# First norm's weights loaded as columns, x scaled and rounded in smaller steps, and the first products taken by two contraction chunks between the turns of x

## What is computed

```python
def rms_norm(x, g):
    xf = x.astype(jnp.float32)
    y = xf * lax.rsqrt(jnp.mean(jnp.square(xf), axis=-1, keepdims=True) + EPS)
    return (y * g.astype(jnp.float32)).astype(x.dtype)
...
qkv_raw, z, b, a, q_down, kv_down, gates = jnp.split(
    rms_norm(x, norm_mix) @ w_in, IN_SPLITS, axis=-1)
```

## Time and profile before

| | |
|---|---|
| median of 3 runs | 1457.36 us (1457.14 to 1457.37) |
| span of the profiled execution | 1455.6 us |
| PE busy | 1445.4 us (99%) |
| ACT busy | 868.4 us (60%) |
| DVE busy | 808.5 us (56%) |
| POOL busy | 217.1 us (15%) |
| granted clock of PE in 40 equal slices | 90% or more in each |
| chain that ended last | PE 96%, DVE 2% |

### The profile page before, as it was taken

One profiled execution on the slowest core, in us unless ns is written; L12 is line 12 of the kernel. 1 busy time (PEld: TensorE's weight loads), 2 busy tenths in 40 slices (PEclk: granted clock), 3 DMA queues, 4 the chain that ended last, 5 costly groups with the idle time before them and its releaser, 6 DMA issues.

```text
span 1455.6 us, 28542 instructions
## 1 busy us (share of the span) xinstructions
PE 1445.4 (99%) x10052; PEld 1182.0 (81%) x10052; DVE 808.5 (56%) x1664; ACT 868.4 (60%) x2816; POOL 217.1 (15%) x111
## 2 busy tenths in 40 slices
PE   9999999999999999999999999999999999999998
PEld 7877777877777777778777787777778999999998
DVE  5865445555546564555655555645434766777643
ACT  5545678686666686575855667766775353344332
POOL 3001111111122111111221111122122000000000
PEclk9999999999999999999999999999999999999999
DMA  9541315653245534365333453333734465555551
GB/s 280 172 119 30 83 26 117 156 116 70 63 102 123 121 86 86 74 132 125 85 70 82 113 139 70 63 70 73 189 77 152 145 235 183 168 172 191 181 174 59
DMA packets 263720, 173.61 MB, mean 119 GB/s; under 512 B 165464, under 2 KB 212088, under 8 KB 263576
## 3 DMA queue, kind: packets, MB, share of 16 engines
q1 hardware_dynamic: 263266, 171.53, 45.3%
q10 hardware_dynamic: 318, 0.33, 0.1%
HBM read 132.22 MB, written 6.74 MB: 95 GB/s over the span
## 4 chain that ended last, share of the span: by engine, by line
PE 96%; DVE 2%; ACT 0%; DMA 0%; ACTq 0%; issue 0%; POOL 0%; DVEq 0%
PE ps L2016 17%; PE ps L2018 16%; PE ps L2017 16%; PE ps L2453 6%; PE ps L2454 6%; PE ps L2455 6%; PE ps L2056 2%; PE ps L2037 2%; PE ps L2109 2%; PE ps L2401 2%; PE ps L2402 2%; PE ps L2110 2%; PE ps L2403 2%; PE ps L2111 2%; PE ps L1894 2%; PE ps L2046 1%
## 5 line engine op out<-in xcount | busy, mean ns | idle before, releaser
L851 ACT ACTIVATE ksq<-ps 128x128 f32<-128x128 f32 x1024 | 268.1, 277 | 279.5 <-PE ps L2018 278.0
L2016 PE MATMUL ps<-ukh,cTh 128*128 128x512 f32 x1024 | 418.4, 409 | 0.3 <-DVE cTl L1236 0.3
L2018 PE MATMUL ps<-ukh,cTl 128*128 128x512 f32 x1024 | 400.7, 391 | 0.0
L2017 PE MATMUL ps<-ukl,cTh 128*128 128x512 f32 x1024 | 399.9, 391 | 0.0
L705 POOL TENSOR_TENSOR rk<-kss,mhalf 128x32 f32<-128x32 f32 x32 | 180.1, 5628 | 478.0 <-DVE kss L1684 478.0
L2016 PEld LDWEIGHTS ps<-ukh,cTh 128*128 128x128 f32 x1024 | 192.6, 188 | 55.8 <-issue 17.1
L2018 PEld LDWEIGHTS ps<-ukh,cTl 128*128 128x128 f32 x1024 | 192.2, 188 | 42.9
L2017 PEld LDWEIGHTS ps<-ukl,cTh 128*128 128x128 f32 x1024 | 192.8, 188 | 34.0
L851 ACT ACTIVATION_READ_ACCUMULATOR ksq<-ps 128x1 f32 x1024 | 212.2, 207 | 0.0
L839 ACT ACTIVATE cTr<-turned 128x1024 uint16<-128x1024 uint16 x126 | 173.8, 1379 | 10.9 <-PE ps L2040 5.7
L1236 DVE TENSOR_TENSOR cTl<-cTr,cTh 128x512 fp32r<-128x512 f32 x128 | 88.4, 691 | 136.9 <-ACT cTh L842 136.0
(11 more groups left out here) (514 smaller groups left out, 2590.7 us busy)
## 6 DMA issues: line engine op xcount, KB each, us to landing
clat<-cache_mla SPq DMA_DIRECT2D x128, 256.0 KB, 2.6
wraw<-w_in SPq DMA_DIRECT2D x16, 1024.0 KB, 5.1
wraw<-w_up SPq DMA_DIRECT2D x16, 1024.0 KB, 5.4
wraw<-w_down SPq DMA_DIRECT2D x16, 1024.0 KB, 5.0
braw<-w_in SPq DMA_DIRECT2D x24, 512.0 KB, 4.0
crope<-cache_mla SPq DMA_DIRECT2D x128, 32.0 KB, 2.4
sst<-state_gdn SPq DMA_DIRECT2D x32, 128.0 KB, 3.2
gdn_sample<-sst SPq DMA_DIRECT2D x32, 128.0 KB, 2.0
```

The source lines that it names most:

```text
L851: i = nc.scalar.activation(ksq[:, P * h:P * h + P], ps[:, k % 3, P * h:P * h + P], ACT.Square, accum_out=kss[:, n // 4 % 2, n % 4, 4 * hal ...
L2016: mm(out, cTh[:, n % 2, c], ukh[:, c, cols], start=c == 0, stop=False)
L2017: mm(out, cTh[:, n % 2, c], ukl[:, c, cols], start=False, stop=False)
L2018: i = mm(out, cTl[:, n % 2, c], ukh[:, c, cols], start=False, stop=c == 3)
```

## The change

Four things are changed, all within the front.

1. `norm_mix` is loaded once more, straight as columns into a small tile `mixp` (128 partitions by 8), by a DMA that ACT issues second. Each of its 1,024 numbers is a piece of 4 bytes by itself. `x_normed` reads `mixp` and no longer `par`.
2. x is scaled and rounded in three steps, of two, two and four chunks (`XQ`), and ACT rounds weight piece 0 in two steps of two contraction chunks each (`first_hi`). `lo(0)` is still one step.
3. PE's order: six chunks of x are turned, then comes one more unused matmul into bank 4, then the high products of half unit 0 for contraction chunks 0 and 1 (`first_products(0)`), then x chunks 6 and 7, then the high products for chunks 2 and 3.
4. The turn of `prow` goes behind those products and waits until ACT has copied chunk 7; its copy to `par` stands on DVE between `x_low(1)` and `lo(1)`.

```diff
@@ ACT
             act.dma_start(consts[:, 0:C_COS.start], C_in[:, 0:C_COS.start]).then_inc(S("consts_landed"), 16)
+            act.dma_start(mixp[:], I["norm_mix"].rearrange("l (c p) -> p (l c)", p=P), allow_slow_non_contiguous=True).then_inc(S("mix_landed"), 16)
...
-            def x_high(half):
-                act.wait_ge(S("x_made"), half + 1)
-                nc.scalar.activation(Ah[:, 4 * half:4 * half + 4, :], xn[:, 4 * half:4 * half + 4, :], ACT.Copy).then_inc(S("left_hi"), 1)
+            def x_high(k):
+                act.wait_ge(S("x_made"), k + 1)
+                nc.scalar.activation(Ah[:, XQ[k], :], xn[:, XQ[k], :], ACT.Copy).then_inc(S("left_hi"), 1)
+
+            def first_hi(kc):
+                act.wait_ge(S("w_landed0"), landed[0])
+                nc.scalar.activation(hi_of(0)[:, kc, :], wraw[:, 0, kc], ACT.Copy).then_inc(S("w_hi0"), 1)
 
             x_chunk(1)
+            first_hi(slice(0, 2))
+            x_high(0)
             x_chunk(3)
-            hi(0)
-            x_high(0)
+            first_hi(slice(2, 4))
+            x_high(1)
+            act.wait_ge(S("w_hi0"), 2)
+            act.sem_inc(S("w_hi"), 1)
             x_chunk(5)
             x_chunk(7)
             hi(1)
...
@@ DVE
+            def x_normed(k):
+                n_ = XQ[k].stop - XQ[k].start
+                v.wait_ge(S("mix_landed"), 16)
+                v.wait_ge(S("x_even"), XQ[k].stop // 2)
+                v.wait_ge(S("x_odd"), XQ[k].stop // 2)
...
             x_chunk(0)
+            x_normed(0)
             x_chunk(2)
-            v.wait_ge(S("side_done"), side("params"))
-            V.tensor_copy(par[:, 0:PR_ALL], ps[:, 4, 0:PR_ALL]).then_inc(S("side_read"), 1)
-            x_normed(0)
+            x_normed(1)
             x_chunk(4)
             x_chunk(6)
             x_low(0)
             lo(0)
-            x_normed(1)
+            x_normed(2)
             x_low(1)
+            v.wait_ge(S("side_done"), side("params"))
+            V.tensor_copy(par[:, 0:PR_ALL], ps[:, 4, 0:PR_ALL]).then_inc(S("side_read"), 1)
             lo(1)
...
@@ PE
+            def first_products(k):
+                pe.wait_ge(S("w_hi0"), k + 1)
+                pe.wait_ge(S("left_hi"), k + 1)
+                for j in range(4):
+                    half_products(0, 0, 0, hi_of, Ah, j, (2 * k, 2 * k + 1))
+
+            def params_turned():
+                pe.wait_ge(S("params_landed"), 16 * 12)
+                pe.wait_ge(S("x_odd"), 4)
+                nc.tensor.transpose(begin("params")[:, 0:PR_ALL], prow[0:PR_ALL, :], ident[0:PR_ALL, 0:PR_ALL]).then_inc(S("side_done"), 1)
+
+            for c in range(6):
+                x_turned(c)
+            mm(ps[:, 4, :], warm[:, 0:P], warm[:, P:P + 512], start=True, stop=True)
+            pe.wait_ge(S("x_even"), 2)
+            pe.wait_ge(S("x_odd"), 2)
+            first_products(0)
+            x_turned(6)
+            x_turned(7)
+            first_products(1)
```

More of the change, by code:

```diff
@@ L257, in build @@
         assert e <= PERSIST
+        mixp, _ = place("mixp", [P, KC], F32, 212800 - 64)
         warm, _ = place("warm", [P, 640], F32, taken["qr"][0])
@@ L449, in z_columns @@
             return 1024 * 3 + 512 * (i // 2) if i < 4 else OFF_GATES + 512 * ((i - 4) // 2)
+        XQ = [slice(0, 2), slice(2, 4), slice(4, 8)]
         SLOT = {0: 0, 1: 1, 3: 0, 6: 1, 7: 0, 8: 1, 9: 0, 10: 1}
@@ L774, in _ @@
             square(sq[:, 0:8, :], xT[:], "sq_ready")
-            x_high(1)
+            x_high(2)
             hi(2)
@@ L800, in _ @@
                 drain(5, j, 12 + j, kn[:, 4 + j, :])
-            act.wait_ge(S("x_made"), 3)
+            act.wait_ge(S("x_made"), 4)
             nc.scalar.activation(rsq[:, 1], rsq[:, 0], ACT.Sqrt).then_inc(S("sqrt_done"), 1)
@@ L1141, in x_chunk @@
                 V.tensor_copy(xT[:, c, :], ps[:, XBANK[c], 0:T]).then_inc(S("x_even"), 1)
[L1143 to L1148, removed]
+            def x_normed(k):
[3 more added lines that the diff above has]
+                v.wait_ge(S("x_odd"), XQ[k].stop // 2)
+                V.tensor_tensor(xn[:, XQ[k], :], xT[:, XQ[k], :], mixp[:, XQ[k]].unsqueeze(2).to_broadcast([P, n_, T]), ALU.mult).then_inc(S("x_made"), 1)
             def x_low(half):
                 cs = slice(4 * half, 4 * half + 4)
-                v.wait_ge(S("left_hi"), half + 1)
+                v.wait_ge(S("left_hi"), half + 2)
                 V.tensor_tensor(Al[:, cs, :], xn[:, cs, :], Ah[:, cs, :].bitcast(F32), ALU.subtract).then_inc(S("left_lo"), 1)
             x_chunk(0)
+            x_normed(0)
             x_chunk(2)
-            v.wait_ge(S("side_done"), side("params"))
-            V.tensor_copy(par[:, 0:PR_ALL], ps[:, 4, 0:PR_ALL]).then_inc(S("side_read"), 1)
-            x_normed(0)
+            x_normed(1)
             x_chunk(4)
@@ L1188, in _ @@
             lo(6)
-            v.wait_ge(S("left_hi"), 4)
+            v.wait_ge(S("left_hi"), 5)
             V.tensor_tensor(qdl[:], qd[:], qdh[:].bitcast(F32), ALU.subtract).then_inc(S("left_lo"), 1)
@@ L1886, in unit, with half_products @@
                         beside(j)
+            def half_products(n, q0, half, w, x, j, kcs=range(4), last=False):
+                for kc in kcs:
+                    i = mm(ps[:, (q0 + j) % 4, 0:T], w(n)[:, kc, 128 * j:128 * j + 128], x[:, 4 * half + kc, :], start=w is hi_of and x is Ah and half == 0 and kc == 0, stop=last and kc == 3)
+                return i
             def half_unit(n, q0, half, beside=None):
[L1890 to L1902, removed]
+                if n > 0:
+                    pe.wait_ge(S("w_hi"), n + 1)
+                    pe.wait_ge(S("left_hi"), half + 2)
+                    for j in range(4):
+                        if half == 0:
+                            bank(q0 + j)
+                        half_products(n, q0, half, hi_of, Ah, j)
                 if beside:
@@ L1906, in half_unit @@
                 for j in range(4):
-                    products(hi_of, Al, j)
+                    half_products(n, q0, half, hi_of, Al, j)
                 pe.wait_ge(S("w_lo"), n + 1)
                 for j in range(4):
-                    products(lo_of, Ah, j, half == 1).then_inc(S("chunk_done"), 1)
+                    half_products(n, q0, half, lo_of, Ah, j, last=half == 1).then_inc(S("chunk_done"), 1)
             pe.wait_ge(S("warm_ready"), 1)
@@ L1916, in _, with x_turned @@
             pe.wait_ge(S("x_landed"), 32)
[L1917 to L1922, removed]
+            def x_turned(c):
                 b = ps[:, XBANK[c]]
```

6 lines of the change are left out of this document (2 added, 4 removed).

## The result

| | before | after |
|---|---|---|
| median | 1458.0 us (1456.5 to 1459.3, 21 runs) | 1459.8 us (1459.4 to 1462.2, 21 runs) |
| ratio after to before | | 1.0016, 95% interval 1.0009 to 1.0022 |
| span of the profiled execution | 1455.6 us | 1460.3 us |

By the ratio the change makes the kernel slower by 2.3 us (1.3 to 3.2 by the interval); the medians differ by 1.8. Each execution has both a time and a span, and the time is 1.8 us the longer of the two. The profiled execution is the slowest of the 21 (1462.16 us). That is 2.4 us more than the span before. What only the first trace shows is therefore not taken for the change's own.

A forecast was written before the change was run, and what follows sets the result against it. PE bounds the kernel, but DVE's `lo(1)` limits the front's gain to 0.57 us. Low weights at 26.9 instead of 25.73, plus 1.2, take the median from 1457.36 to 1458.6 us; range 1456.5 to 1460.5.

The forecast's parts named there:

- plus 1.2: Forecast sum: PE starts the low weights of half unit 1 at 26.9 instead of 25.73, delay passing to the end.
- `mixp` late: Rival at DVE's first scaling: `mixp` lands beyond 12.8, or late together with low clock; plus 4.1 at 14; chance 0.11.
- the likeliest case: In the front: full PE clock with ACT waiting for the weight, plus 0.6 to 1.9 us; chance 0.45.
- mixp in time: ACT's added column load: `mixp` lands before DVE wants it at 9.2.
- my two bounds: Landing of `mixp`: 5.5 us if its packets go in a row, 11.2 if each lets one 2 KB packet by.
- The price of lateness: Front, behind the landing of `mixp`: `x_low(0)` starts 3.75 us after it, instead of at 14.85.
- ACT's order: ACT waits for the weight until 10.8 before copying chunk 3; PE then waits 1.2 us in place of 0.86.
- the DMA's 0.6: Added load's packets on full DMA engines: everything behind pays 0.6 us, first `w_in` piece at 10.8 instead of 10.2.
- the order's 0.6: Front: the plus 0.6 us that would remain if the weight landed at 10.2 all the same.
- DVE bounds the front: Half unit 1's low weights: `lo(1)` ends at 25.16, so PE can gain only 0.57 us before waiting for DVE.
- The lock between POOL and DVE: Front: POOL and DVE exclude each other per instruction; `x_low(1)` takes 2.29 instead of 1.26, `lo(1)` 3.43 instead of 2.29.
- the filler holds it at 12 us: Unused matmul after six turned chunks keeps PE's clock full; rival that it falls: plus 1.8 to 3.0, chance 0.31.

The follow-up runs named there:

- the second trace: The changed kernel traced once more, as it is: 1459.85 us, span 1458.0.
- no_load: Changed kernel without the column load, `mixp` filled with ones by DVE: 1457.77 us, ratio 0.9997.
- rows: Changed kernel with `norm_mix` loaded as 8 contiguous rows of 512 bytes, turned by PE and copied to `mixp` by DVE: 1457.45 us, ratio 0.9998.
- rows_x3: `rows` with ACT's copy of x chunk 3 ahead of the first half of weight piece 0: 1458.04 us, ratio 0.9997.
- split: Changed kernel with the column load cut in two, columns 0 and 1 second in ACT's queue, the other six last: 1462.11 us (one run).
- load_alone: Kernel before plus only the column load as ACT's second DMA, read by no engine: 1462.5 us, ratio 1.0031.
- rows_x3_sq: `rows_x3` with ACT's squares of x placed behind the rounding of x's second half: 1457.43 us, ratio 0.9997.
- rows_x3_pool: `rows_x3` with POOL's first sum of squares held back until `lo(1)` is done: 1460.46 us, ratio 1.0014.

## Why the prediction was right or wrong

The time, 1459.8, lies in the range and 1.2 above the forecast, and the change counts as no change by the 2.9 us bound. Half of the 1.2 is the base: the forecast added its plus 1.2 to a median of 3 runs, 1457.36, and 21 runs give 1458.0. But the delay came by way of a rival, `mixp` late, that the likeliest case had excluded, and "`mixp` awaited on DVE" was one of the signs named as proving the prediction wrong. That the time came so near is in good part luck.

**The step that failed is "mixp in time".** `mixp` was expected by 9.2 and landed at 12.7 in both traces. Of my two bounds the upper one, one 2 KB packet let by for each element, was the right mechanism: it reckoned 98 ns a turn, and 104 are measured. Its 11.2, or 11.6 with the receipt, was 1.1 short. Of that the 64 turns hold 0.4 (6.7 us instead of 6.3), and the rest lies ahead of them and behind them. I chose the lower end because two thirds of the stretch lay ahead of 9.2, which is no argument on the mechanism.

I also leant on an estimate of below 2 us. The Trainium skill, page "DMA: Bandwidth & Descriptors", section "Queues, rings and completion order", states that an engine changes queues after some 9 to 17 descriptors. The estimate applied that to the small packets only and let a single 2 KB packet by at each of the 4 to 8 turns. Applied to both queues, with 89 ns for each 2 KB packet, it is an estimate of 3 to 12 us, so the page gave no ground for "in time". Nor do the packets of this case agree with the figure: their start times (80 to 110 ns from one small packet to the next of an engine) show one for one, and the measurement decides. The Trainium skill's rule on the same page, section "Rules for kernel authors", against a last dimension that is not contiguous was the one to follow.

**The price of lateness was nearly right.** From the landing I had 3.75 us to `x_low(0)`. In the second trace it is 12.68 to 16.42, 3.74. In the first it is 4.61, because the clock fell during the eight products (1.84 us instead of 1.22), ahead of chunks 6 and 7. From there to the end of `lo(1)` I had 12.0 us; it is 11.57 in both traces and 11.41 without the load (13.96 to 25.37), against 11.43 before. So the copy to `par` and the shifted meeting with POOL cost at most 0.14, and not 0.6. By the rival's sum this landing gives plus 2.8; the second trace has plus 2.3 at the low weights (28.04 against 25.73), the medians differ by 1.8, and the ratio gives 2.3.

**ACT's order.** I charged the wait for the first weight with 1.2 us by way of chunk 3's copy. The wait was there (1.37 us; 1.6 forecast), but `w_in` came with 8.7 us after 8.5, not 9.1, and with the load gone nothing was left to pay: `x_low(0)` at 13.96 against 13.73, in an execution whose turns of x began 0.3 us later (7.96 against 7.67). Two terms of my plus 1.2, the DMA's 0.6 and the order's 0.6, were thus each sized too high, and the term put at nothing, the wait for `mixp`, was larger than both. The errors partly cancelled.

**DVE bounds the front: right, and shown.** In `no_load`, `rows` and `rows_x3` PE is rid of its pauses and of the slow clock, and waits 1.11 to 1.15 us for `lo(1)`. Their times are those of before. **The lock between POOL and DVE: right, and shown** by holding POOL back (2.29 to 1.26, 3.22 to 2.28 us). The Trainium skill, page "SBUF — State Buffer", section "Who interferes with whom", states such a lock for the whole instruction, and these lengths agree. The prediction claimed more than its rows give when it said that all four ends fit to 0.1 us: its own figures end POOL's second step at 23.1 by one way and 22.9 by the other, and the rows do not show that end.

**The clock.** That the filler holds it at 12 us was right. I had made that the whole question; in fact it fell 3 to 4 us later, behind PE's wait for the late load. The fall in the front comes with the late load in both traces and is absent in `no_load` and `rows`; by their mean clock, nine of the 21 executions were without it. The fall at 56 us in the slowest execution stays open. PE stands still 1.8 us for POOL just ahead of it, but does so in every trace looked at, and the clock falls there only in this one and in that of `split`.

**The turn of `prow`.** I hid it at no cost, which is right: no wait is shown at L1943. Left where it was, it would have waited for its rows until 15.4 (`load_alone`).

## What to carry to other kernels

In these traces a load whose elements are single descriptors paid, for each, one packet of what the other queue had in flight. So count the elements per DMA engine, multiply by that queue's packet time, and load rows and turn them if the product is not well below the time until use. Before opening up a stretch of one engine, look at who would be late next: here 3.8 us of pause and slow clock on PE were worth nothing, since DVE ended only 0.57 us ahead. When a contended helper is held back to free the critical engine, follow what waits for the helper, since its delay comes back there.

## What was unexpected of the hardware

- 4 KB in 4-byte elements took 11.5 us from issue to landing beside a full queue, and 8.5 us when issued first; 1 MB beside it took 8.7. The small packets passed at 151 to 164 a microsecond beside 2 KB packets, at 77 beside 4 KB ones, and at 764 when the other queue was thin.
- Loads behind such a load in the same queue are held as well: the last row of `prow` came at 15.4 instead of 10.6 us.
- Where POOL became ready during a DVE step, the next DVE step took 4.48 and 4.50 us for a `lo` of 2.28 (`rows_x3_sq`, `rows_x3_pool`), as if it had to let a whole step of POOL by.
- The same program lost the clock at 14.8 us in one execution and at 16.0 in another, and near 56 us in one of the two. Nine of its 21 executions show a mean clock of 1.000, and are at most 0.4 us below the median.
